# Forty-four of the first block's expert rows summed by GpSimd inside the second pass

## The reference, cut to what matters

```python
def one_block(args):                      # 128 tokens at a time, two blocks
    xb, eb, gb = args                     # tokens, chosen experts (128 per token), gates
    h = gelu(einsum('td,ted->te', xb, expert_u[eb]))
    return einsum('te,ted->td', gb * h, expert_v[eb])
```

## Time and profile before

| what | value |
|---|---|
| median of three runs | 3145.84 us |
| the profiled execution | 3145.48 us |
| its span, first to last instruction | 3143.6 us |
| PE / DVE / ACT / POOL busy | 2694.7 / 1272.7 / 426.7 / 803.9 us |
| moved by DMA | 1096.41 MB, 349 GB/s over the span |
| DMA in the tail (2300 to 3086 us) | 421 GB/s, share 1.01 |

### The profile page before, as it was taken

The page is one execution under the profiler, slowest core; times in us unless marked ns, Lnnn a source line. Parts: engine busy times, 40 slices in busy tenths (PEclk is TensorE's granted clock), DMA queues, the critical chain, the costliest instruction groups (busy, mean ns, idle before and its releaser), DMA issues. The chain is left out here.

```text
span 3143.6 us, 37681 instructions
## 1 busy us (share of the span) xinstructions
PE 2694.7 (86%) x16328; PEld 2218.2 (71%) x16328; DVE 1272.7 (40%) x1693; ACT 426.7 (14%) x916; POOL 803.9 (26%) x536
## 2 busy tenths in 40 slices
PE   8899999998999999999898986788766767676566
PEld 7898899998889899889898885788422223222222
DVE  0122001010100155734443455447677775655654
ACT  1121100021000111111101210101100001211121
POOL 0000000000000011212211232233466565555652
PEclk9999999999999999999999988899888888888899
DMA  8976378776837799998998989999999999999996
GB/s 326 305 267 227 136 296 298 285 296 228 311 138 287 260 363 385 354 369 344 424 424 357 383 321 423 420 396 425 409 421 422 421 421 421 421 422 421 422 422 280
DMA packets 126932, 1096.41 MB, mean 349 GB/s; under 512 B 13440, under 2 KB 22064, under 8 KB 28080
## 3 DMA queue, kind: packets, MB, share of 16 engines
q1 hardware_dynamic: 50512, 542.08, 44.3%
q0 software_dynamic: 76256, 551.94, 42.9%
HBM read 1084.52 MB, written 9.44 MB: 348 GB/s over the span
## 5 line engine op out<-in xcount | busy, mean ns | idle before, releaser
L601 PE MATMUL PS<-arena 128*128 128x128 f32 (+1 forms) x13952 | 1883.7, 297 | 78.4 <-DMA arena<-units 64.5
L601 PEld LDWEIGHTS PS<-arena 128*128 128x128 f32 x13952 | 1798.6, 194 | 158.5 <-DMA arena<-units 57.7
L949 PE MATMUL PS<-arena 128*128 128x512 f32 x1152 | 628.6, 706 | 275.8 <-DMA arena<-peer_v,arena 264.2
L949 PEld LDWEIGHTS PS<-arena 128*128 128x128 f32 x1152 | 254.1, 228 | 649.3 <-issue 591.8
L1382 DVE CUSTOM_DVE_ANT_0 arena<-arena 128x2048 f32<-128x2048 f32 x256 | 586.8, 2292 | 287.5 <-DMA arena<-peer_u,arena 281.0
L566 POOL DMA_INDIRECT arena<-peer_u,arena x256 | 399.1, 1559 | 892.5 <-DVE arena L1382 678.2
L566 POOL DMA_INDIRECT arena<-peer_v,arena x256 | 393.8, 1538 | 449.3 <-PE PS L949 214.2
L1392 DVE SCALAR_TENSOR_TENSOR arena<-arena 128x2048 f32<-128x2048 f32 x112 | 263.4, 2352 | 132.0 <-DMA arena<-peer_v,arena 128.7
L972 ACT ACTIVATE arena<-PS 128x512 f32<-128x512 f32 (+2 forms) x154 | 84.5, 549 | 1313.5 <-PE PS L601 1199.9
L1347 ACT ACTIVATE arena<-arena 128x128 f32<-128x128 f32 x144 | 57.9, 402 | 722.9 <-PE PS L949 721.5
L537 POOL DMA_DIRECT2D arena<-ln_rows x2 | 1.3, 640 | 384.7 <-DVE arena L1727 384.7
(11 more groups left out here) (186 smaller groups left out, 1049.0 us busy)
## 6 DMA issues: line engine op xcount, KB each, us to landing
arena<-units SPq DMA_DIRECT2D x243, 2048.0 KB, 9.1
arena<-w_ukv SPq DMA_DIRECT2D x16, 512.0 KB, 10.4
arena<-ln_rows SPq DMA_DIRECT2D x6, 1024.0 KB, 14.8
arena<-ln_rows POOLq DMA_DIRECT2D x4, 1024.0 KB, 18.6
arena<-peer_u,arena POOLq DMA_INDIRECT x256, 23.5
arena<-peer_v,arena POOLq DMA_INDIRECT x256, 23.8
rb_scratch<-arena POOLq DMA_DIRECT2D x1, 3072.0 KB, 38.5
arena<-rb_scratch SPq DMA_DIRECT2D x12, 256.0 KB, 9.8
```

The source lines that it names most:

```text
L601: ins = mm(bank[:, first:first + rhs.shape[1]], lhs, rhs, start=k == 0, stop=k == KT - 1)
L949: ins = mm(Y[c], diag[:, n % 4 * P:(n % 4 + 1) * P], rows[b][:, c * 512:(c + 1) * 512], start=n == first_used[tb], stop=False, skip_group_ ...
```

## The change

`SOON` goes from 28 to 44 and the pattern in the second pass from one V per two U to one V per U, from U72 to U115. GpSimd sums these 44 V itself, in the same instruction stream as the gathers: with a lag of four entries (`LAG`) it waits for the row to land, multiplies it in place by its gate (`tensor_scalar`), waits for its own semaphore, and adds it to the sum (`tensor_tensor`). VectorE sums none in the second pass: its `turn` takes U entries only, most `turn(4)` become `turn(3)` (the one at the second norm goes), and the gates of the first 56 experts are made ready by a fixed call before the attention groups. In the tail VectorE adds its own rows to GpSimd's sum once that is done; the last four V of a block are no longer all the matrix engine's; and instead of four matmuls with VectorE's sum, VectorE adds each PSUM bank to its sum before the statistics of the last norm. In the tail the choice of the next head's experts comes every six U, not every eight.

```diff
-SOON = (NE - FIRST) // 2
+SOON = 44
-LAST = 4
+LAG = 4
...
 def on_vector(s):
     if s < SOON:
-        return True
-    if s % NE >= NE - LAST:
         return False
     return s % 2 == 1 if s >= NE + 64 else s % 3 == 2
...
         order.append(("U", e))
-        if e >= FIRST and (e - FIRST) % 2:
-            order.append(("V", (e - FIRST) // 2))
+        if FIRST <= e < FIRST + SOON:
+            order.append(("V", e - FIRST))
...
+                elif before[1] < SOON:
+                    pool.wait_ge(added, before[1] + 1)
...
-            for kind, s in ARRIVALS:
+            def add_row(s):
+                b, nth, _ = ROWS["V", s]
+                if s == 0:
+                    pool.wait_ge(begun, 1)
+                    pool.wait_ge(gated, 1)
+                else:
+                    pool.wait_ge(added, s)
+                pool.wait_ge(row_landed[b], 16 * (nth + 1))
+                nc.gpsimd.tensor_scalar(rows[b], rows[b], gates[0][:, s:s + 1], None, ALU.mult).then_inc(scaled_row, 1)
+                pool.wait_ge(scaled_row, s + 1)
+                nc.gpsimd.tensor_tensor(acc, acc, rows[b], ALU.add).then_inc(added, 1)
+
+            for n, (kind, s) in enumerate(ARRIVALS):
                 gather(kind, s)
+                if n >= LAG and ARRIVALS[n - LAG][0] == "V" and ARRIVALS[n - LAG][1] < SOON:
+                    add_row(ARRIVALS[n - LAG][1])
...
-                if e == NE - LAST:
-                    pe.wait_ge(v_summed, summed_to(s))
-                    for c in range(4):
-                        ins = mm(Y[c], ident, sums[tb][:, c * 512:(c + 1) * 512], start=False, stop=False, skip_group_check=True)
-                    ins.then_inc(all_summed, 1)
...
+                elif summed_to(s) == 1:
+                    dve.wait_ge(added, SOON)
...
-                end = min(at[0] + n, LATE)
-                for kind, s in ARRIVALS[at[0]:end]:
-                    if kind == "U":
-                        dot(s)
-                    else:
-                        if s == 0:
-                            gate(0)
-                        add_row(s)
+                end = min(at[0] + n, NE)
+                for e in range(at[0], end):
+                    dot(e)
...
                 for c in range(4):
+                    link(v.tensor_tensor(parts[c], parts[c], banks[c], ALU.add))
                     link(v.bn_stats(stats[:, 48 + 6 * c:54 + 6 * c], parts[c]))
```

More of the change, by code:

```diff
@@ L138, in used_to @@
 def used_to(s):
-    return s + 1 - summed_to(s)
+    return s + 1 - SOON - summed_to(s)
 def arrivals():
@@ L394, in trunk_layer @@
         dot_done, gelu_done, v_summed, v_used = (sem(n) for n in ("dot_done", "gelu_done", "v_summed", "v_used"))
-        gated, all_summed = sem("gated"), sem("all_summed")
+        gated, begun, scaled_row, added = (sem(n) for n in ("gated", "begun", "scaled_row", "added"))
         gh_done, diag_done = sem("gh_done"), sem("diag_done")
@@ L1690, in trunk @@
                 if tb:
-                    turn(4)
+                    turn(3)
                 gated_sums(q)
                 if tb:
-                    turn(4)
+                    turn(3)
                 normed_out(q)
                 if tb:
-                    turn(4)
+                    turn(3)
                 for s in range(8):
@@ L1713, in trunk @@
                 groups = 4 * (tb + 1)
+                if tb:
+                    gate(0)
                 next_biases(tb, 0)
@@ L1747, in trunk @@
                 second_norm(tb)
-                if tb:
-                    turn(4)
                 choose(tb, 0)
                 final_rows(tb)
-                link(v.tensor_scalar(sums[tb], h_tok[tb], ALPHA, None, ALU.mult))
+                mark(v.tensor_scalar(sums[tb], h_tok[tb], ALPHA, None, ALU.mult), begun, tb + 1)
             trunk(0)
@@ L1758, in _, with last_norm @@
             trunk(1)
-            turn(LATE)
+            turn(NE)
             gate(1)
-            def last_norm(tb, parts, done):
+            def last_norm(tb, banks, done):
+                parts = [sums[tb][:, c * 512:(c + 1) * 512] for c in range(4)]
                 for c in range(4):
+                    link(v.tensor_tensor(parts[c], parts[c], banks[c], ALU.add))
                     link(v.bn_stats(stats[:, 48 + 6 * c:54 + 6 * c], parts[c]))
@@ L1780, in _ @@
                     dot(s)
-                    if s % 8 == 1 and s // 8 - NE // 8 < PEER_HEADS - 1:
-                        choose(1, s // 8 - NE // 8 + 1)
+                    k, more = divmod(s - NE, 6)
+                    if more == 1 and k < PEER_HEADS - 1:
+                        choose(1, k + 1)
                 else:
@@ L1786, in _ @@
                     if s == NE + PK:
-                        dve.wait_ge(all_summed, 1)
                         dve.wait_ge(v_used, used_to(NE - 1))
@@ L1791, in _ @@
                         add_row(s)
-            dve.wait_ge(all_summed, 2)
             dve.wait_ge(v_used, used_to(TB * NE - 1))
```

## The result

The changed kernel takes 3390.84 us in the median of four runs (3390.02 to 3391.42) against 3145.51 us for the kernel before beside it: a ratio of 1.0779, 95% interval 1.076 to 1.0798, or 245 us more. The forecast was 3277 us with a range to 3375 us: the direction and the mechanism hold, the size doesn't, and the measured time lies beyond the range. The profiled execution has a span of 3388.3 us.

What follows compares the result with a forecast made beforehand. GpSimd's new block of 11.34 us was taken to bound the second pass: 201 - 10 - 62 + 5 - 3 = +131 us on the profiled 3145.48 us, so 3277 us, with an 8 in 10 range of 3128 to 3375 us.

Steps and rivals of the forecast that it cites:

- The bound: Second pass: GpSimd needs 1.6 times what the pass gives it, so VectorE is late in nearly every turn; 60 in 100.
- The block: GpSimd, second pass: U gather, V gather, scale and add, each waiting for the one before: 11.34 us, 7.8 to 15.0.
- twice VectorE's time, 7.04 us: GpSimd's scale and add in a block, taken as twice VectorE's 1.23 plus 2.29 us.
- The upper bound of 10.7 us: GpSimd's scale and add: VectorE's 3.52 us times 3.05, the factor by which its company stretches a gather.
- The lateness: Turn behind cross attention head 2, with U116's dot: ends at 2270 us where before it was 2069, 201 us late.
- the 41 of the working: Second pass, blocks 3 to 43: one microsecond more or less in the block moves the forecast by 41 us.
- What comes back: Behind head 2: -10 us rest of pass, -62 us for 25 rows landed earlier, +5 us tail start, -3 us end.
- -10 us in the rest of the pass: Second pass without V gathers: PE's waits for `vc_scratch` and `keys_cols`, 5.6 + 4.7 us, go.
- 5 us for the start of the tail: Just before the tail: the slots stand full and DMA starts up again from there, costing +5 us.
- GpSimd keeping up: Rival, second pass: scale and add take 3.5 to 3.8 us, GpSimd no bound, at best 3118 us; 13 in 100.
- The landing: Rival, `add_row`: waiting for a V issued two blocks ago keeps blocks at least 9.8 us, 3214 us; 12 in 100.
- The lock: Rival, second pass: VectorE's dot and GpSimd's add can't run together, 13.6 us a block, 3371 us; 15 in 100.

Runs made afterwards that it cites:

- no sums: The changed kernel with the 44 V rows gathered at the same places but neither scaled nor added, a slot free once its row has landed: 3158.35 us.
- the new list and the old slots: Kernels with the changed kernel's 44 V order, without the follow-up edit sending the six entries behind the pass to row slots; changed kernel 3390.84 us, with that edit 3375.17.
- the kernel with 28 V: The changed kernel with the old list, 28 V, one behind every second U, still scaled and added by GpSimd: 3231.31 us, ratio 1.0274.
- The product: The changed kernel with GpSimd's scale written as a multiplication of two tensors, the gate repeated along the row: 3340.39 us, ratio 1.0619.

## Why the prediction was wrong, and where it was right

**The bound: right.** GpSimd's block was named as the bound and VectorE's in-order turns as the way in which it reaches the matrix engine. POOL at 557 of 581 us, VectorE's 385 us of waiting for `peer_u` and PE's waits for VectorE are that chain, and cutting either half of the block gives three quarters of the loss back.

**The block: mis-sized, 11.34 against 13.75 us.** This is the step that failed. The gathers were well taken (3.10 against 2.92), my waits too large (1.2 against 0.58). The failed term is "twice VectorE's time, 7.04 us" for scale and add: it is 10.25 us. The add is 2.05 times VectorE's 2.29 us, as I had it. The scale is 4.5 times VectorE's 1.23 us. On VectorE the scale takes half as long as the add, on GpSimd (5.55 against 4.70 us) it takes longer than the add, so VectorE's row of the scale was the wrong base. Measured against the two-input row both GpSimd operations are 2.1 to 2.4 times as long. The upper bound of 10.7 us held, by little. The estimate of 6.2 us from the GPSIMD Engine Reference of the Trainium skill (Performance versus the Vector engine) erred the same way and further: its 4497 ns for an add agrees with the 4.49 to 4.53 us seen undisturbed, its near one element per cycle for one input, by an estimate 1.8 us, does not agree with 5.46.

**The lateness: 201 us forecast, 290 measured.** U116's gather starts at 2349.34 us and not at 2253. The turn behind head 2 ends at 2359.4 us, and before it was 2069. 41 blocks of 2.4 us more are 98 us. The chain started 7 us earlier, the first block took 5 us more (its scale alone 6.71 us), and from U116's gather to its dot's end it was 10 us and not 17, since the landing was nearer 8 than 13 us: 98 - 7 + 5 - 7 = 89 us more. Across the runs the pass's lateness follows the block as measured: 105 us at 9.6 us a block, 102 at 9.5, 244 at 12.6 and 290 at 13.75. From the shortest to the longest that is 45 us for each microsecond, near the 41 of the working. But the lateness ends at 58 us, not at zero, when GpSimd has no arithmetic at all (no sums). I compared with the pace of before and left out that 30 more gathers had to fit between the groups and head 2: 30 x 2.49 = 75 us of transfer into 22 us of room, 53 us too many, which is the lateness behind head 2 in that run. In the changed kernel this floor is not reached, since DMA moves only 264 GB/s there.

**What comes back: 70 us forecast, 46 measured.** I expected -10 us in the rest of the pass; it is nothing, the pass ends 290 us late. From the pass's end to the end of the span before needs 923.7 us and the changed kernel 878.1: 46 us less, where I had 62 - 5 + 3 = 60. No row landed through the weight ring before the pass ended, since its first free place came at 2509 us, so 22 rows more had landed, not 25, and 5 us for the start of the tail was too little: 22 x 2.49 = 55 us, 5 us gained at the end, and so 14 us lost in between. 131 + 89 + 10 + 14 = 244 us, which is the measured 245.

**The step that was missing.** The working priced the rows that are fetched earlier, but not what DMA does when the list is used up and the pass goes on. That is 45 us of empty DMA time in 2397 to 2509 us, present with 37 to 47 us in every kernel with the new list and the old slots. It is not 45 us on top of the 244, but a part of the same loss, seen from the side of the DMA engines.

**The rivals.** GpSimd keeping up is out. Its gain was not there to be had either: with no arithmetic at all on GpSimd the time is 3158 us, not 3118. The landing sets the block only when the arithmetic is cut. The lock exists, but it isn't the reason for 3391 being nearer to its 3371 than to my 3277. VectorE in order of time in the changed kernel, two dots in a row:

```profile
1793.79 2.29 DVE L1391 CUSTOM_DVE_ANT_0 arena<-arena 128x2048 f32<-128x2048 f32 x1
...
1796.12 6.49 DVE L1391 CUSTOM_DVE_ANT_0 arena<-arena 128x2048 f32<-128x2048 f32 x1
```

and GpSimd beside it:

```profile
1788.75 5.46 POOL L580 TENSOR_SCALAR arena<-arena 128x2048 f32<-128x2048 f32 x1
1794.29 6.18 POOL L582 TENSOR_TENSOR arena<-arena 128x2048 f32<-128x2048 f32 x1
```

The add that starts inside the first dot takes 6.18 us, 1.65 more than its 4.53; the second dot, which starts inside the add, ends at 1802.6 us, 2.1 after the add. One waits for the other nearly whole, as SBUF — State Buffer of the Trainium skill (Who interferes with whom) has it for a VectorE instruction with two inputs against a GpSimd one that reads. But it adds little to the block, and mostly at another place than I looked: 20 of the 42 U gathers take 2.86 us and not 0.99, nearly all of them behind an add for which a dot had waited. On average the U gather is 1.90 us where it is 1.20 without sums, and the add 4.70 us and 4.53 alone. That is 0.9 us of 13.75, by the slope of 42 some 37 us of the time as an estimate, and the gathers' part stood in my averages already. What it stretches is VectorE, which waits for rows anyway: the dots of that stretch take 3.28 us and not 2.29.

## What to carry to other kernels

When work moves to an engine that also feeds a queue, price one round of its new loop, measure that loop against the pace at which an in-order consumer asks for its rows, and multiply the shortfall by the rounds. Take the price of an operation from a row of the engine that will run it. Where there is none, take the row with two tensors as the base: the row of the scale, doubled, was still too low here by a factor of 2.3. And where a stream is brought forward on a nearly full DMA, count the bytes that must fit between the same two landmarks, and ask what the DMA has left to do when the stream is used up before its stage ends: the sum of empty DMA time showed in every run where the loss lay, though not why.

## What was not expected of the hardware

- GpSimd's scale of 128x2048 float32 by a scalar takes 5.46 us undisturbed, the multiplication of two tensors 3.61 and the add of two 4.5. By a constant the scale is hardly faster (5.39 to 5.40).
- Scale and add differ in how they hold up a dot. One that starts inside the add ends 2.15 us behind it, as if it had begun when the add ended. One that starts in the first 3.5 us of a scale ends 0.42 us behind it (0.3 us into a scale, a dot took 5.55 us in the kernel with 28 V; 3.4 us into one, 2.48 us in the changed kernel). So it does not wait for the scale's last part, and the add behind it takes 4.70 us. The product leaves no such gap: the dot then meets the add, and this is where the average of 5.51 us comes from.
- A small VectorE scale of 128x256 in cross attention, 0.35 us before, took 6.17 us on average in the changed kernel, between GpSimd's sums:

```profile
L1683 DVE TENSOR_SCALAR arena<-arena 128x256 f32<-128x256 f32 x3 | 18.5, 6171 | 0.1
```
